# One-hots of the gate spread: columns batched on VectorE, rows shared with GpSimd

## The reference, cut to what matters

```python
expert = (jnp.take_along_axis(i1, top_c // PEER_TOPK, axis=-1) * PEER_N_KEYS
          + jnp.take_along_axis(i2, top_c % PEER_TOPK, axis=-1))
gate = jax.nn.softmax(top_s, axis=-1)

def expert_block(args):
    xb, eb, gb = args
    act = jax.nn.gelu(jnp.einsum("pd,ped->pe", xb, jnp.take(u, eb, axis=0)), approximate=False)
    return jnp.einsum("pe,ped->pd", (gb * act).astype(v.dtype), jnp.take(v, eb, axis=0))
```

## Time and profile before

| | us |
|---|---|
| median of 3 runs | 5225.89 (5223.86 to 5232.66) |
| the profiled execution | 5221.33, of it 5220.0 span |
| spread stage in it, first one-hot to last store issued | 1278.6 to 1413.7 |

### The profile page before, as it was taken

How to read it: one execution, slowest core, us unless ns; L and a number is a source line. 1 busy time by engine, 2 the same in 40 slices (tenths; PEclk the granted TensorE clock), 3 DMA queues, 4 the chain that set the end, 5 groups by cost and what they waited for, 6 DMA issues and landing times.

```text
span 5220.0 us, 67116 instructions
## 1 busy us (share of the span) xinstructions
PE 4890.2 (94%) x27321; PEld 4127.0 (79%) x27321; DVE 3112.8 (60%) x5380; ACT 1926.7 (37%) x2848; POOL 1264.5 (24%) x1009
## 2 busy tenths in 40 slices
PE   7998989998799999999899898999999899889999
PEld 7887878788689999997677786788888577667787
DVE  4544455779757999986433535356666444454545
ACT  3445522234833333333432415223223443342332
POOL 1111000036745666652210012100000210020000
PEclk8998999999999999999999999999999999999999
DMA  4111114422568999983001010123322111113222
GB/s 159 49 53 58 41 56 154 161 86 86 213 233 316 344 346 347 346 313 139 26 29 62 17 63 17 57 81 121 109 110 99 41 50 53 45 38 105 81 97 73
DMA packets 157154, 636.29 MB, mean 122 GB/s; under 512 B 12352, under 2 KB 62544, under 8 KB 106288
## 3 DMA queue, kind: packets, MB, share of 16 engines
q1 hardware_dynamic: 112528, 467.97, 24.7%
q0 software_dynamic: 42240, 160.88, 8.3%
q10 hardware_dynamic: 2080, 3.15, 0.2%
HBM read 595.25 MB, written 36.70 MB: 121 GB/s over the span
## 4 chain that ended last, share of the span: by engine, by line
PE 81%; DVE 9%; ACT 5%; DMA 2%; issue 2%; POOL 1%; DVEq 0%; ACTq 0%; SPq 0%; POOLq 0%
PE banks L269 68%; PE banks L2966 2%; PE banks L2971 1%; PE banks L3065 1%; DVE cols L2997 1%; ACT P L3015 1%; PE banks L3092 1%; PE banks L1022 1%; DVE oa L2275 1%; DMA X<-ctxT_in 1%; PE banks L395 1%; PE banks L954 1%; PE banks L348 1%; PE banks L1013 1%; ACT high L203 1%
## 5 line engine op out<-in xcount | busy, mean ns | idle before, releaser
L218 DVE TENSOR_TENSOR low<-raw,high 128x2048 fp32r<-128x2048 f32 (+2 forms) x333 | 736.7, 2213 | 697.9 <-ACT high L203 674.0
L269 PE MATMUL banks<-UH,high 128*128 128x512 f32 (+2 forms) x2784 | 1017.3, 365 | 45.4 <-DVE UL L510 11.8
L269 PE MATMUL banks<-UL,high 128*128 128x512 f32 (+2 forms) x2784 | 1003.1, 360 | 0.0
L269 PE MATMUL banks<-UH,low 128*128 128x512 f32 (+2 forms) x2784 | 1002.7, 360 | 0.0
L203 ACT ACTIVATE high<-raw 128x2048 fp32r<-128x2048 f32 (+3 forms) x341 | 619.9, 1818 | 656.7 <-PE banks L269 294.3
L269 PEld LDWEIGHTS banks<-UH,high 128*128 128x128 f32 (+1 forms) x2784 | 526.0, 189 | 146.0 <-issue 41.2
L269 PEld LDWEIGHTS banks<-UH,low 128*128 128x128 f32 (+1 forms) x2784 | 526.8, 189 | 87.2
L269 PEld LDWEIGHTS banks<-UL,high 128*128 128x128 f32 (+1 forms) x2784 | 526.3, 189 | 82.9 <-issue 0.7
L269 PE MATMUL banks<-UpH,high 128*128 128x384 f32 (+1 forms) x1152 | 396.5, 344 | 5.8 <-POOL low L231 4.9
L269 PE MATMUL banks<-UpH,low 128*128 128x384 f32 (+1 forms) x1152 | 395.4, 343 | 0.0
L269 PE MATMUL banks<-UpL,high 128*128 128x384 f32 (+1 forms) x1152 | 395.3, 343 | 0.0
(11 more groups left out here) (423 smaller groups left out, 9868.7 us busy)
## 6 DMA issues: line engine op xcount, KB each, us to landing
raw<-uT_in SPq DMA_DIRECT2D x64, 1024.0 KB
raw<-ev_in SPq DMA_DIRECT2D x64, 1024.0 KB
raw<-up_in SPq DMA_DIRECT2D x44, 1024.0 KB
raw<-ada_in SPq DMA_DIRECT2D x40, 1024.0 KB
gd<-stage SPq DMA_DIRECT2D x12, 2048.0 KB, 6.8
gt<-gd SPq DMA_DIRECT2D x32, 768.0 KB, 12.9
side<-ada_in SPq DMA_DIRECT2D x24, 1024.0 KB, 10.0
raw<-gate_in SPq DMA_DIRECT2D x24, 1024.0 KB
```

The lines of the kernel that those rows point to most:

```text
L218: v.e.tensor_tensor(k.low[j % RAW][:, 0:w], k.raw[j % RAW][:, 0:w], k.high[i % SPL][:, 0:w].bitcast(F32), ALU.subtract).then_inc(*v.inc("w ...
L269: ins = pe.e.matmul(out, x, y, start=start and i == 0 and j == 0, stop=stop and i == n - 1 and j == 2)
```

## The change

- DVE makes column one-hots for the tokens of a group of four in one instruction, a comparison of two tensors: iota repeated n times against n columns of k.e2T, each repeated 128 times. n is 4 in the first group of a round and 3 in the other three, so 13 columns of 16 in 4 instructions. The slots of ob become slices of one tensor, so that the output is one range.
- ACT makes the columns of 3 tokens in 16 (t % 16 = 7, 11, 15), in place of 5.
- POOL makes no columns; it makes the row one-hots of 7 tokens in 16 with the two-operation instruction, and DVE those of the other 9. They count on semaphores of their own, hot_pool and hot_a.
- A column instruction waits until PE has done the matmul of the last of its tokens 16 before, so up to three slots are held a little longer.

```diff
+    k.obs = m.sb("ob", [128, NOH * 128])
+    k.ob = [k.obs[:, i * 128:(i + 1) * 128] for i in range(NOH)]
...
-def expert_engine(t):
-
-    if t % 16 in (1, 5, 7, 11, 13):
-        return "act"
-    return "dve" if t % 16 in (3, 8, 14) else "pool"
+def row_engine(t):
+
+    return "pool" if t % 16 in (1, 3, 5, 8, 10, 12, 14) else "dve"
+
+
+def column_engine(t):
+
+    return "act" if t % 16 in (7, 11, 15) else "dve"
...
+def one_row(e, k, t):
+    return e.e.tensor_scalar(k.oa[t % NOH][:], k.iota[:], k.e1T[:, t:t + 1], k.gT[:, t:t + 1], ALU.is_equal, ALU.mult)
...
+        group = range(4 * q, 4 * q + 4)
+        ts = [t for t in group if column_engine(t) == "dve"]
+        n, t = len(ts), ts[0]
         if t >= NOH:
-            v.wait_ge("mm", ("hot", t - NOH))
...
+            v.wait_ge("mm", ("hot", ts[-1] - NOH))
+        ob = k.obs[:, t % NOH * 128:(t % NOH + n) * 128].rearrange("p (t e) -> p t e", e=128)
+        v.e.tensor_tensor(ob, k.iota[:].unsqueeze(1).to_broadcast([128, n, 128]), spread(k.e2T[:, t:t + n], 128), ALU.is_equal).then_inc(
+            *v.inc("hot_dve", *ts))
+        for t in group:
+            if row_engine(t) == "dve":
+                if t >= NOH:
+                    v.wait_ge("mm", ("hot", t - NOH))
+                one_row(v, k, t).then_inc(*v.inc("hot_a", t))
...
     for t in range(TD):
-        if expert_engine(t) == "pool":
+        if row_engine(t) == "pool":
             if t >= NOH:
                 g.wait_ge("mm", ("hot", t - NOH))
-            g.e.tensor_scalar(k.ob[t % NOH][:], k.iota[:], k.e2T[:, t:t + 1], None, ALU.is_equal).then_inc(*g.inc("hot_pool", t))
+            one_row(g, k, t).then_inc(*g.inc("hot_pool", t))
```

More of the change, by code:

```diff
@@ L1769, in peer_plan @@
     k.oa = [m.sb("oa", [128, 128]) for _ in range(NOH)]
-    k.ob = [m.sb("ob", [128, 128]) for _ in range(NOH)]
+    k.obs = m.sb("ob", [128, NOH * 128])
+    k.ob = [k.obs[:, i * 128:(i + 1) * 128] for i in range(NOH)]
     k.stage = [m.sb("stage", [128, 128, BT]) for _ in range(2)]
@@ L2231, in spread_pe @@
             t = 4 * q + i
-            pe.wait_ge("hot_a", t)
-            if expert_engine(t) == "act":
+            if row_engine(t) == "pool":
+                pe.wait_ge("hot_pool", t)
+            else:
+                pe.wait_ge("hot_a", t)
+            if column_engine(t) == "act":
                 pe.wait_ge("hot_act", t)
-            elif expert_engine(t) == "dve":
+            else:
                 pe.wait_ge("hot_dve", t)
-            else:
-                pe.wait_ge("hot_pool", t)
             ins = pe.e.matmul(b[:, i * 128:(i + 1) * 128], k.ob[t % NOH][:], k.oa[t % NOH][:], start=True, stop=True)
@@ L2271, in spread_dve @@
     v.wait_ge("chosen", ("T", 2))
-    for t in range(TD):
+    for q in range(TD // 4):
+        group = range(4 * q, 4 * q + 4)
+        ts = [t for t in group if column_engine(t) == "dve"]
+        n, t = len(ts), ts[0]
         if t >= NOH:
-            v.wait_ge("mm", ("hot", t - NOH))
[L2275 to L2278, removed]
+            v.wait_ge("mm", ("hot", ts[-1] - NOH))
[7 more added lines that the diff above has]
+                one_row(v, k, t).then_inc(*v.inc("hot_a", t))
     v.mark("spread")
```

## The result

| | us |
|---|---|
| before, median of 8 runs | 5226.93 (5222.61 to 5232.66) |
| after, median of 8 runs | 5256.69 (5247.39 to 5272.51) |
| ratio after / before | 1.0059, 95% interval 1.0045 to 1.0072 |

The account below looks back on a forecast made before the run. ACT was taken to bound the spread stage at 5.56 us a round. Afterwards POOL's 4.48 plus 0.54 of waits makes it 5.0, so 22.9 rounds save 12.8 us: 5213 us, range 5203 to 5246.

Parts of the forecast that it names:

- What bounds the kernel now: In the spread stage before the change, ACT is the bound: 5.52 us of work in a 5.56 us round.
- ACT, PE, DVE afterwards: In a round after the change, ACT needs 4.08 us, PE 4.08 and DVE 4.5 to 5.0.
- POOL's second operation: In POOL's row one-hots the second operation adds nothing; seven instructions at 0.64 us take 4.48 a round.
- rival B: POOL's second operation costs over 0.14 us extra (e): round 5.02 + 7e, up to 5265 us in all; 17%.
- The waits behind comparisons: POOL's instructions, starting at random, wait behind DVE's two-tensor comparisons: 0.077 us each, 0.54 a round.
- Rival D: Nothing measurable: second operation costs 0.02 to 0.14 us, or lock waits bunch (1.73 us); rounds 5.1 to 6.0; 28%.
- The waits on small instructions: POOL's 0.64 us an instruction, taken from the kernel before, includes the waits that DVE already causes there.
- The head of the stage: At the stage's start PE, below full clock, limits the first 18 tokens, so only 22.9 rounds change.
- Rival C: A comparison waits for a whole POOL instruction, so they never overlap: 6.2 us a round, 5241 in all; 10%.

Follow-up runs that it names:

- The table's lower right corner: The changed kernel with one operation in POOL's row one-hots and DVE's columns made one by one: stage 118.4 us.
- the two better kernels: The changed kernel with POOL making 4 rows and ACT 4 columns of 16, ratio 0.9965; the kernel before with one column moved from ACT to DVE, 0.9980.

## Why the prediction was wrong

**What bounds the kernel now: right.** ACT at 5.52 us of a 5.56 us round. One column moved from ACT to DVE and nothing else gave 9 us of the stage.

**ACT, PE, DVE afterwards: right.** DVE's rows 0.26 apart, comparisons at 0.55 and 0.69 us; the group wait costs nothing. The table's lower right corner, 118.4 us, is near the 120 that the forecast meant for the stage (132.9 less 12.8), but it is no check of the forecast's waits: there POOL's instruction has one operation and no comparison beside it, and waits beside small instructions come to about the same sum by chance.

**POOL's second operation: the step that failed.** The bounds were nothing and 0.32 us, and the low end was taken "because the row nearest in its number of operations is the cheap one". That row, L1196, has two constants; the new instruction has two scalars from memory. It was nearer to L3050 and L2289, which have one and cost 2.5 ns an element, and from which only the high end followed. Measured: 0.19 at rest, of it in the kernel before 0.115 for the operation and 0.075 for its scalar in memory. By the prediction's own formula, 5.02 + 7 x 0.19 = 6.35 us a round, rival B with 18 us slower. The rule between two far bounds is to take the row nearest in what makes the price, and here DVE's 60 ns for the same step was a warning that was filed under rival B only.

**The waits behind comparisons: right in kind, 2.5 times too small in size.** The lock of rows 8 is what the changed kernel shows, and 0.54 us a round was worked out for it from random starts of zero length. Measured is 1.37. The average was wrong in two ways. First, the length: a POOL instruction is held until 0.52 us behind the start of a 128x384 comparison (0.18 + 0.35, 0.31 + 0.21) and 0.67 behind that of a 128x512 one (0.19 + 0.48), where 0.40 and 0.53 had been worked out from the price of an element. By the prediction's own formula these lengths give 7 x (0.67^2 + 3 x 0.52^2) / (2 x 5.0) = 0.88 us. Second, starts are not random: comparisons follow matmuls that wait for POOL's rows, and each of the four comparisons of a round catches a POOL instruction, 0.48 + 2 x 0.35 + 0.21 = 1.39. Rival D had named this bunching (1.73 us at the worst) and given it no price of its own together with B. Both happened at once: 7 x 0.775 + 1.37 = 6.8. **That two rivals could hold together, each with its price, was left out of the range.** Together they give (6.8 - 5.56) x 24 = 30 us, the result.

**The waits on small instructions: no part of the loss.** POOL's 0.64 an instruction carried the waits of the kernel before over. In the changed kernel the three instructions that no comparison holds take their free 0.79. Only with the columns one by one do such waits count, 0.12 us in the median, with two operations on POOL (0.901 against 0.784) as with one (0.713 against 0.592).

**The head of the stage: too cautious.** It was said that PE limits the first 18 tokens in any case. Before, PE did 20 records from its start without a gap (rows 14); in the changed kernel it does 11 and then waits for a row of POOL's:

```profile
1278.99 3.25 PE L2244 MATMUL banks<-oa,ob 128*128 128x128 f32 x11 [3.75 <-DVE oa L2274]
```

With a POOL one-hot every 0.97 us, POOL limits the first tokens too, and 24 rounds lose, not 22.9.

**Rival C: wrong.** No comparison of the changed kernel waited for POOL. The Trainium skill (SBUF — State Buffer, section "SBUF: two separate sides") has the shared ports taken by whichever starts first, for the whole instruction, and the other fully blocked. Where the POOL instruction starts second the trace agrees: it waits for the end of the comparison. Where the comparison starts second it agrees only in part: by the records, one that starts up to 0.21 us into a POOL instruction goes first, one at 0.25 waits 0.10, and one at 0.45 runs beside it with no wait for either (the run with the rows first). A record's start need not be the moment at which the ports are taken, and no run here shows that moment; but POOL's instruction of 0.79 us does not keep a comparison out for its whole length.

## What to carry to other kernels

When work moves to the slowest engine, price the exact instruction there, its operations and where each scalar comes from; a neighbour with fewer of either is no estimate of it. A batched instruction with two tensor inputs on DVE saves DVE time and charges it to POOL, up to about its own length for each POOL instruction that it meets. Here it paid to give POOL no more instructions than there are batches, or to leave the batches out. Put rivals that can hold together into the range as a sum.

## What the runs showed of the hardware

On POOL a 128x128 is_equal against a scalar from memory takes 0.597 us, with a multiplication by a constant 0.712, with one by a scalar from memory 0.787. On DVE the last costs 0.34 in place of 0.28.

POOL's two-operation instruction waits behind DVE's comparisons for about what is left of them: 0.48 us behind one of 128x512 that started 0.19 ahead, 0.54 behind one of 128x384 that started 0.21 into it. The comparison waits only when it starts near 0.25 us into POOL's instruction (0.65 in place of 0.55); at 0.45 and at 0.60 us into it the two run side by side, and only the next POOL instruction pays.

The time of the whole program varies with TensorE's granted clock outside the stage. The profiled span of the changed kernel is 5246.1 us at a mean clock of 0.974, that of the kernel without comparisons 5243.5 at 0.970. The stage of the second is 13.2 us shorter, its span only 2.6: what lies behind the stage took 3804.3 us in the one and 3814.3 in the other, for the same instructions. The same stretch of time in both, which by then lies within some 3 us of the same place in the program, shows the clock, 0.99 against 0.93:

```profile
4600.00:4720.00 120.00, 103.88 (x772) 79.08 (x770) 65.95 (x175) 56.98 (x129) 34.06 (x25) 0.99 0.10 33
```

```profile
4600.00:4720.00 120.00, 104.88 (x751) 78.80 (x750) 65.36 (x180) 56.07 (x131) 31.36 (x20) 0.93 0.06 18
```

It is no property of one kernel: of ten runs with 5 rows on POOL, two took 5218 to 5219 us at a mean clock of 0.974 and eight 5229 to 5237 at 0.968 to 0.971, and the 15 runs of before beside one set of experiments go from 5217.9 at 0.973 to 5232.7 at 0.968. What decides between them was not found. It is why the experiments are read by the stage and the two better kernels by 7 to 9 runs each.
